# Odd mixer's HGRN products: 128 by 128 matmuls against 32 by 32 matmuls in four column groups of TensorE

## The reference, cut to what matters

```python
def gla_chunkwise(q, k, v, log_g):
    def step(s_st, inp):
        qb, kb, vb, gb = inp
        bc = jnp.cumsum(gb, axis=2)
        diff = bc[:, :, :, None, :] - bc[:, :, None, :, :]
        wdec = jnp.exp(jnp.where(mask, diff, -jnp.inf))
        att = jnp.einsum('bhtk,bhtsk,bhsk->bhts', qb, wdec, kb)
        ...
o_f = gla_chunkwise(qh, heads(1.0 - f_f), vh, heads(jnp.log(f_f)))
o_b = _flip_l(gla_chunkwise(_flip_l(qh), _flip_l(heads(1.0 - f_b)), _flip_l(vh), _flip_l(heads(jnp.log(f_b)))))
```

## Time and profile before

| | |
|---|---|
| profiled execution | 2541.97 us |
| its span | 2540.2 us |
| PE busy | 2478.7 us (98%) |
| PE weight loads busy (beside PE) | 2050.9 us (81%) |
| DVE busy | 1328.6 us (52%) |
| POOL busy | 1052.5 us (41%) |
| ACT busy | 900.8 us (35%) |
| DMA | 219.37 MB, 86 GB/s |

### The profile page before, as it was taken

One profiled execution on the slowest core, in us unless ns is written; L12 is line 12 of the kernel. 1 busy time (PEld: TensorE's weight loads), 2 busy tenths in 40 slices (PEclk: granted clock), 3 DMA queues, 4 the chain that ended last, 5 costly groups with the idle time before them and its releaser, 6 DMA issues.

```text
span 2540.2 us, 32332 instructions
## 1 busy us (share of the span) xinstructions
PE 2478.7 (98%) x11654; PEld 2050.9 (81%) x11654; DVE 1328.6 (52%) x1547; ACT 900.8 (35%) x1171; POOL 1052.5 (41%) x484
## 2 busy tenths in 40 slices
PE   8999999998998999999999999999999999999998
PEld 7888886766777888888888888888888887888887
DVE  3333448997777333245333335667877456433335
ACT  3223237775444222214222225445444323322212
POOL 6444443332235444445444445333333334444443
PEclk9999999998999999999999999999999999999999
DMA  5333222221122333322333332222222222233322
GB/s 166 92 98 103 97 82 65 73 70 50 59 61 72 99 93 97 108 92 74 99 98 92 105 111 75 75 75 68 75 75 75 67 83 75 83 99 91 110 92 79
DMA packets 63769, 219.37 MB, mean 86 GB/s; under 512 B 10920, under 2 KB 15016, under 8 KB 63552
## 3 DMA queue, kind: packets, MB, share of 16 engines
q1 hardware_dynamic: 63120, 216.03, 27.0%
q0 software_dynamic: 560, 2.11, 0.2%
HBM read 216.02 MB, written 2.10 MB: 86 GB/s over the span
## 4 chain that ended last, share of the span: by engine, by line
PE 87%; DVE 6%; ACT 4%; issue 2%; POOL 1%; DMA 0%; ACTq 0%; DVEq 0%; POOLq 0%; SPq 0%
PE ps L505 24%; PE ps L507 24%; PE ps L506 24%; PE ps L957 2%; PE ps L536 2%; DVE sb_th L1798 1%; ACT sb_wh L1131 1%; PE ps L487 1%; PE ps L662 1%; PE ps L661 1%; PE ps L660 1%; PE ps L666 1%; PE ps L488 1%; PE ps L493 1%; DVE sb_x L1694 1%
## 5 line engine op out<-in xcount | busy, mean ns | idle before, releaser
L414 POOL TENSOR_TENSOR sb_wl<-sb_raw,sb_wh 128x1024 fp32r<-128x1024 f32 (+1 forms) x376 | 979.3, 2605 | 1414.7 <-ACT sb_wh L1131 1414.7
L1131 ACT ACTIVATE sb_wh<-sb_raw 128x1024 fp32r<-128x1024 f32 (+1 forms) x376 | 419.1, 1115 | 1340.6 <-PE ps L507 1274.6
L505 PE MATMUL ps<-sb_xh,sb_wh 128*128 128x512 f32 x2096 | 829.8, 396 | 1.0 <-DVE sb_rq L2042 0.5
L507 PE MATMUL ps<-sb_xl,sb_wh 128*128 128x512 f32 x2096 | 816.3, 389 | 0.0
L506 PE MATMUL ps<-sb_xh,sb_wl 128*128 128x512 f32 x2096 | 816.0, 389 | 0.0
L505 PEld LDWEIGHTS ps<-sb_xh,sb_wh 128*128 128x128 f32 x2096 | 393.8, 188 | 84.6 <-issue 4.9
L507 PEld LDWEIGHTS ps<-sb_xl,sb_wh 128*128 128x128 f32 x2096 | 393.4, 188 | 83.0
L506 PEld LDWEIGHTS ps<-sb_xh,sb_wl 128*128 128x128 f32 x2096 | 393.8, 188 | 81.7 <-issue 3.1
L1606 DVE SCALAR_TENSOR_TENSOR sb_hf<-sb_sg,ps 128x512 f32<-128x512 f32 x88 | 60.5, 687 | 589.2 <-PE ps L507 565.0
L505 PE MATMUL ps<-sb_hh,sb_wh 128*128 128x512 f32 x616 | 239.7, 389 | 0.8 <-POOL sb_wl L414 0.8
L507 PE MATMUL ps<-sb_hl,sb_wh 128*128 128x512 f32 x616 | 239.7, 389 | 0.0
(11 more groups left out here) (336 smaller groups left out, 2956.0 us busy)
## 6 DMA issues: line engine op xcount, KB each, us to landing
sb_raw<-w_in SPq DMA_DIRECT2D x176, 512.0 KB, 3.5
sb_raw<-w_out SPq DMA_DIRECT2D x64, 704.0 KB, 4.0
sb_raw<-w_od SPq DMA_DIRECT2D x80, 512.0 KB, 3.5
sb_raw<-w_ev SPq DMA_DIRECT2D x40, 512.0 KB, 3.5
sb_raw<-w_evo SPq DMA_DIRECT2D x8, 512.0 KB, 3.5
sb_raw<-w_odo SPq DMA_DIRECT2D x8, 512.0 KB, 3.4
sb_x<-x_in SPq DMA_DIRECT2D x8, 256.0 KB, 6.5
out<-sb_x SPq DMA_DIRECT2D x16, 128.0 KB, 1.8
```

The source lines that it names most:

```text
L414: pool.tensor_tensor(wl[:, sl.par, 0:n], raw[:, sl.par, 0:n], wh[:, sl.par, 0:n].bitcast(F32), ALU.subtract).then_inc(lo_done, 1)
L505: pe.matmul(out, w_h, rh(k), start=start and k == 0, stop=False)
L507: mm = pe.matmul(out, w_h, rl(k), start=False, stop=stop and k == kt - 1)
L1131: act.activation(wh[:, sl.par, 0:kt * P], raw[:, sl.par, 0:kt * P], ACT.Copy).then_inc(hi_done, 1)
```

## The change

The four matmuls of 128 by 128 at the diagonal and at each level become matmuls on the parts of the square that the masks can read. With W = 32 for the diagonal and the levels 0 to 5 and W = 64 for level 6, the keys of W positions (the loaded weights, W columns) meet the queries of W positions (streamed), and the result goes to the partitions y to y + W of the bank. For levels 5 and 6 the queries are those of the neighbouring square (`y ^ (1 << l)`). The rest of the bank keeps what it held. Waits, semaphores and the order of all other work are as before.

```diff
+CW = 32
...
                     for b_ in range(NB):
-                        c = slice(b_ * P, (b_ + 1) * P)
-                        mm = pe.matmul(ps[:, 5, c], ks[:, c], hq[:, c], start=True, stop=True)
+                        for y in range(0, P, CW):
+                            c = slice(b_ * P + y, b_ * P + y + CW)
+                            mm = pe.matmul(ps[y:y + CW, 5, c], ks[:, c], hq[:, c], start=True, stop=True)
                     mm.then_inc(a_diag_mm, 1)
...
+                        W = max(CW, 1 << l)
                         for b_ in range(NB):
-                            c = slice(b_ * P, (b_ + 1) * P)
-                            mm = pe.matmul(ps[:, 6 - l % 2, c], KQ[:, l % 2, 0, c], KQ[:, l % 2, 1, c],
-                                           start=True, stop=True)
+                            for y in range(0, P, W):
+                                o = b_ * P
+                                t0 = o + (y ^ (1 << l) if 1 << l >= CW else y)
+                                mm = pe.matmul(ps[y:y + W, 6 - l % 2, t0:t0 + W], KQ[:, l % 2, 0, o + y:o + y + W],
+                                               KQ[:, l % 2, 1, t0:t0 + W], start=True, stop=True)
                         mm.then_inc(a_lv_mm, 1)
```

## The result

The changed kernel takes 2525.22 us (median of 4 runs, 2522.95 to 2526.88), the kernel before 2542.31 beside it (4 runs, 2541.55 to 2543.68): ratio 0.9931, 95% interval 0.9918 to 0.9944, so 17.1 us less. Forecast were 2528.6 us, 14.4 less, in a range from 2521 to 2565. A later series of 5 runs of the same kernel gave 2524.43 against 2541.61 (9 runs), ratio 0.9934 (0.992 to 0.9947).

What follows compares the result with a forecast made beforehand. PE was taken to bound the odd mixer's heads, so block savings enter the span directly. Gains of 1.2 + 0.58 + 0 = 1.8 us a head, x 8 = 14.4, gave 2543.0 - 14.4 = 2528.6 us, range 2521 to 2565.

Steps and rivals of the forecast that it cites:

- What bounds the kernel: Odd mixer's eight heads: PE busy 395.22 of 399 us, so time gained in a block enters the span one to one.
- In and out: Edges of each small-product block: 0.12 us going in and 0.20 coming out, 0.32 together, bounds 0 to 0.40.
- Inside: Within a 32-wide block: four column groups side by side, 8 passes each at 0.041 us, 0.33 us a block.
- weight-path rival: All blocks: groups share one weight-load path, loads still take 0.89 us, excursions add 18 us: 2561; chance 0.25 with shared start gap.
- Levels 1 to 5: Level product blocks: 0.65 us in place of 0.89, 0.24 gained each, 1.2 us a head.
- Diagonal and level 0: Head's first two blocks, sharing one entry and exit: 0.58 us gained, 0.2 lost to level 0's wait for ACT's copy.
- Level 6: 64 by 64 products in two groups: 8 passes at 0.066 us, 0.15 in, 0.20 out; 0.88 for 0.89, no gain.
- What is late next: Level 1's products wait for the diagonal's masked copy on DVE, with 0.36 us to spare after the 0.58 gain.
- a new wait of L957 for ACT or DVE: Sign of being wrong: the level products on PE newly waiting for ACT or DVE; no size given.
- The sum: Eight heads: 1.2 + 0.58 + 0 = 1.8 us a head, 14.4 us in all, 2543.0 to 2528.6.
- the floor for each pass: Rival, all blocks: no overlap, 32 passes at 0.062 us, 1.98 inside; 80 us slower, 2623; chance 0.10.
- Partial overlap: Rival, all blocks: two groups at a time at best, 0.56 us inside; 2.9 us gained, 2540.1; chance 0.12.

## Why the prediction was right

*What bounds the kernel.* PE's time went into the span one to one, as said: the blocks' savings sum to 17.9, the stretch shrank by 17.5, the time by 17.1.

*In and out.* 0.32 estimated from row groups; 0.33 measured for an extra excursion. 0.09 us is the pause in both. This term was read from the nearest rows, and right for the reason given.

*Inside.* 0.33 estimated with 0.041 a pass. From the changed kernel's block: 0.59 - 0.32 = 0.27. In it the starts within a group lie 0.032 apart, record by record, nearer the bound of 0.028 than I put it, and 0.02 goes to the fourth group's later start. This is the term that was mis-sized most: some 0.065 x 5 levels x 8 heads = 2.6 us.

That the groups work side by side at all was a bet at 0.53: no row showed column groups. It was won in part by luck, since the edit happens to alternate the groups in the program, and the prediction neither asked for that order nor had a rival without it. With the loops exchanged the inside is 0.70, between the forecast and the weight-path rival, and the change loses time.

*Levels 1 to 5.* 1.54 a head for 1.2.

*Diagonal and level 0.* 0.64 gained for 0.58, in heads 1 to 7 with the wait for ACT's copy in it, as forecast; in head 0 the copy is early and the gain is 0.89, which was not seen.

*Level 6.* 0.08 for 0. The entry was right: the first load starts 0.09 behind the stream (1702.94 to 1703.03) and takes some 0.05 (the first matmul's record, 0.270, is that much longer than the 0.222 of those behind), 0.14 in all for the 0.15 put down, and 0.20 out was right too. The pass was put too high, 0.066 where the trace has 0.058: behind the first one, two more matmuls, one a group, start every 0.06 us.

```profile
1703.03:1703.15 0.12, 0.12 (x4) 0.12 (x6) 1.00 0.00 0
1703.03:1703.33 0.30, 0.30 (x10) 0.30 (x12) 1.00 0.00 0
```

0.81 - 0.14 - 0.20 = 0.47, and 8 x 0.058 = 0.46; forecast were 0.53.

*What is late next.* In heads 1 to 6 the diagonal's copy ends 0.25 to 0.30 ahead of level 1's first load, where 0.36 was worked out. Head 7 was not looked at: it has one tile of projection less behind level 0, and there the wait costs 0.55 us. Among the signs of being wrong stood "a new wait of L957 for ACT or DVE"; this is one, of a size that does not change the forecast.

*The sum.* 14.4, and 2.6 for the inside of levels 1 to 5, 0.7 for the diagonal and level 0 (7 x 0.06 + 0.31), 0.7 for level 6, less 0.5 for head 7, make the 17.9 of the blocks. The errors nearly all lie on one side.

*The rivals.* One weight path and the floor for each pass are out: four loads run at once. Partial overlap is out for this order of the passes, but the exchanged loops show it: 0.70 inside, and the time then lies above that of the kernel before. The rule that a weight load overlaps matmuls in flight only when the row group differs (the Trainium skill, TensorE: Matmul & The Clock Gate, Part 3, What overlaps and what doesn't) does not hold for column groups here: loads of different groups, all over the same 128 rows, run beside matmuls. Nor does the start gap of about 25 ns (same page, Part 1) hold across groups: 32 matmuls start within 0.26 us, 0.008 apart; within one group they are 0.032 apart, which does not contradict it.

## What to carry to other kernels

If masks read only squares along the diagonal of a product, products of 32 by 32 in four column groups do the same useful work in less than a third of the time inside (0.27 for 0.89), but each excursion from the whole array into groups and back costs 0.33 us. So small products should stand together. An estimate from these two numbers: a block shrinks to 0.3 of its time and pays 0.33, so one that takes under some 0.47 us in the whole array gains nothing. The order of the passes matters as much as their size: neighbouring matmuls must go to different groups, or the kernel ends slower than it began (2551.42 us for 2538.73). When a block on PE shrinks, look at its first instance in a loop and its last, where less other work stands ahead of the next wait.

## What the runs showed of the hardware that was not expected

A column group takes waiting passes ahead only a little: with eight passes of one group in a row, the next group starts with three of the eight not yet begun, 0.153 us behind with 32 columns a pass and 0.29 us behind with 64. Doubling loads and columns of a pass to 64 takes the step between a group's starts from 0.032 to 0.058, less than twice; with 32 loaded and 64 streamed it is 0.056. A group's first step is longer than those behind it, 0.05 and 0.11 for 32 and 64 columns; its first load has no stream to run beside.
